# One order of work for the attention stage: mix, halves, late tiles and rotation move

## The chip, the cores and the metric

The kernel runs on one core of a Trainium2 chip. The metric is the device time of one execution in microseconds; before the change it is 2108.4 us, the median of three runs (2104.35 to 2110.85). Nothing about the result is known where this part of the document was written.

## The reference

Two layers of a hybrid decoder. Each normalises x, projects it with one matrix, runs sliding window attention (group A) and retention (group B) beside each other, gates both and projects back. Only group A matters here. Cut to that:

```
h = rms_norm(x, norm_g);  p = h @ w_in                      # 2048 prompt rows + 32 sample rows
qa = rotary(rms_norm(qa, q_norm_g), pos, 16, 500000)        # 8 heads of 64
ka = rotary(rms_norm(ka, k_norm_g), pos, 16, 500000)        # 2 heads of 64
s  = (qa @ ka.T) * 64 ** -0.5, masked to a window of 128    # own block and the one before
p  = exp(s - m) / (sum(exp(s - m)) + exp(sink - m))
attn = p @ va;   mixed = concat(silu(ga) * attn, ...)       # x = x + mixed @ w_out
```

## The kernel before

A layer has four stages in time: A, B0, B1 (two heads of the retention each) and O (the projection back). Each goes over 17 steps, one of 32 sample rows and 16 tiles of 128 prompt rows. Every product of the projections is made of three f16 products (a high part and a low part of each operand), so every operand is written twice: by ScalarE (ACT) the high part, by another engine the low part. Every engine has its own order of instructions, written out by hand, and semaphores between them. The A stage of layer 0 also makes the tiles of h that are missing at its start.

In step s of stage A the engines hold three tiles at once: s is projected, t = s-1 gets its scores and softmax, u = s-2 its product with v and its gate ("mix"). In one step:

- TensorE (PE) runs `proj` in three pieces (q of 512 columns, k and v of 256, gate of 512), 24, 24 and 24 matmuls. In between stand `a_T` (transposes of q and k of t, 18 matmuls into piece 0), `a_S` for both key groups (in the middle of piece 1), `a_PV(u,0)` (before piece 2) and `a_PV(u,1)` (18 matmuls into piece 2). `a_T` waits for the rotated q and k (`a_qk`), and for both mixes of the tile before (`a_mx`), because it writes into the bank TK that the second mix reads.
- ScalarE copies the transposed q and k as f16 (`a_tout`), takes squares of q (`a_q`) and k (`a_kv`), the exponentials of both halves (`a_exp`), the high parts of the probabilities (`a_phi`), of v (`a_vhigh`) and the tanh of the gate (`a_tanh`). That last one waits for `a_mx` too.
- VectorE (DVE) follows with `gate`, the low parts (`a_plo` of the probabilities, `a_vlow` of v, `a_lo` of q and k), `a_land_q` and `a_land_k` (q and k out of PSUM), `a_softmax(t,0)` and `(t,1)` (mask, maximum), the twelve links of the reciprocal root (`a_norm_link`), `a_rotate` and the two mixes.
- SyncE (SP) issues the DMAs: `prob_T(s,g)` transposes the probabilities of half g (it waits for `a_plo`), `store_mix` writes the mix, `p_T(n)` transposes tile n of h. `a_softmax(t,1)` waits (`a_tp`) until `prob_T(u,1)` has landed, since it writes where that transposition reads from.
- GpSimd (POOL) issues the loads of the weights, does the reduction of a maximum over partitions (`share_max`), and in layer 0 the low parts of the tiles 4 to 16 of h (`late_low`). `load_weights` and `share_max` stand between them.

In steps 8 to 15 ("weight steps") DVE and ACT also split the next weights: `w_high` and `w_low`, two each in a step. Steps 4 to 6 have maxima of these weights (`w_absmax`, then `w_top`) at their end. The others are called plain here. In the trace, DVE's L1004 is `gate`, L1017 `a_plo`, L1010 `a_vlow`, L930 `a_land_q`, L1051 the mask of the softmax, L972 the scaling at the head of `a_rotate`, L981 to L984 its rotation, L889 `w_low`, L1112 the mixes; PE's L569 and L571 are `a_T`, L605 `a_S`, L645 `a_PV`; POOL's L1988 and L1990 are `late_low`; SP's L2097 is `prob_T`, L2057 `store_mix`, L2089 `p_T`; ACT's L1788 is the high part of a tile of h.

## Time and profile before

| | |
|---|---|
| median of three runs | 2108.4 us |
| the profiled execution | 2112.67 us |
| its span, first to last instruction | 2110.7 us |
| busy: PE, DVE, ACT, POOL | 1837.4, 1407.4, 715.7, 134.4 us |
| mean granted TensorE clock | 0.947 |
| stage A of layer 0 and of layer 1 | some 65 to 515 us, some 1140 to 1520 us |

Busy time is a share of the span and says nothing of what an engine waits for. A row of a timeline is one instruction or several merged ones, and where the engine was idle before it the row ends with that time and with whoever released it. Outside stage A the order of no engine changes.

### The profile page before, as it was taken

What the parts mean: (1) busy time and instruction counts of PE and PEld (TensorE: products, weight loads), DVE (VectorE), ACT (ScalarE), POOL (GpSimd) and SP (SyncE); (2) the same over time, 40 slices, a digit from 0 to 9 for tenths busy, and PEclk for the clock granted to TensorE, in tenths of its full rate; (3) what the DMA queues carried; (4) which work ended last, traced back from release to release, by engine and by line L of the source; (5) the groups of instructions that cost most, each with busy time, mean ns of one, the idle gap of its engine ahead of it and who ended that gap; (6) DMA issues with size and microseconds to landing.
All of it is one profiled execution on the core that took longest, in us unless ns stands there. A gap on an engine that the chain in (4) does not pass through costs nothing.

```text
span 2110.7 us, 36140 instructions
## 1 busy us (share of the span) xinstructions
PE 1837.4 (87%) x11752; PEld 1004.8 (48%) x11752; DVE 1407.4 (67%) x4699; ACT 715.7 (34%) x1809; POOL 134.4 (6%) x134
## 2 busy tenths in 40 slices
PE   0787677795899999997899988898599999999999
PEld 0344344453455555553344555454255555555444
DVE  4768577783666576667786799888376657667442
ACT  2544344452122222222243455555112222232110
POOL 3221122101000000003001000001000000000000
PEclk9888888898899999999999999999799999999999
DMA  5953233327200120019999133234610021002874
GB/s 148 226 137 70 51 73 75 71 59 169 77 11 10 64 88 12 10 41 252 223 247 232 22 76 75 56 68 87 121 49 13 10 92 59 10 12 77 189 216 148
DMA packets 353803, 196.64 MB, mean 93 GB/s; under 512 B 296624, under 2 KB 327536, under 8 KB 353552
## 3 DMA queue, kind: packets, MB, share of 16 engines
q1 hardware_dynamic: 343984, 159.89, 32.6%
q0 software_dynamic: 9728, 35.66, 5.4%
q8 instruction: 42, 0.69, 0.1%
q14 instruction: 49, 0.40, 0.1%
HBM read 88.75 MB, written 41.16 MB: 62 GB/s over the span
## 4 chain that ended last, share of the span: by engine, by line
PE 53%; DVE 19%; DMA 8%; issue 6%; ACT 3%; SPq 3%; POOL 2%; DVEq 1%; ACTq 0%; POOLq 0%
PE PB L515 22%; PE PA L515 21%; DMA r<-r 5%; DVE r L1051 3%; DVE mix L1112 2%; PE S L669 1%; PE OB L688 1%; PE TK L658 1%; PE S L704 1%; PE OB L695 1%; DVE r L1017 1%; DVE land L972 1%; POOL hT L1988 1%; DMA hT<-land 1%; DVE w_mx L872 1%
## 5 line engine op out<-in xcount | busy, mean ns | idle before, releaser
L515 PE MATMUL PA<-w_a,hT 128*128 128x512 f16 (+1 forms) x1920 | 416.0, 368 | 18.2 <-DVE land L1004 16.9
L515 PE MATMUL PB<-w_a,hT 128*128 128x512 f16 (+1 forms) x1920 | 422.3, 372 | 8.1 <-DVE land L946 4.6
L515 PEld LDWEIGHTS PB<-w_a,hT 128*128 (+1 forms) x1920 | 190.5, 102 | 200.5 <-issue 30.8
L515 PEld LDWEIGHTS PA<-w_a,hT 128*128 (+1 forms) x1920 | 189.2, 101 | 199.4 <-issue 20.9
L515 PE MATMUL PA<-w_b,hT 128*128 128x512 f16 x768 | 184.4, 392 | 21.5 <-DVE land L1004 21.5
L515 PE MATMUL PA<-w_b,r 128*128 128x512 f16 x768 | 174.9, 385 | 24.0 <-DMA r<-r 15.1
L515 PE MATMUL PB<-w_b,hT 128*128 128x512 f16 x768 | 180.8, 386 | 3.9 <-DVE r L1141 3.9
L1680 ACT ACTIVATE r<-r,nm,unqk 128x256 f32<-128x256 f32 x256 | 149.9, 589 | 67.3 <-DVE sd L1064 67.3
L515 PE MATMUL PB<-w_b,r 128*128 128x512 f16 x768 | 171.3, 379 | 0.0
L1745 ACT ACTIVATE r<-OB 128x128 f32<-128x128 f32 (+1 forms) x136 | 36.3, 272 | 390.5 <-PE S L704 364.1
L1161 DVE TENSOR_TENSOR r<-S,t_dec 128x256 f32<-128x256 f32 x64 | 27.2, 424 | 159.1 <-PE S L669 158.9
L515 PEld LDWEIGHTS PA<-w_b,r 128*128 128x128 f16 x768 | 75.1, 99 | 119.9 <-DMA r<-r 24.3
L515 PEld LDWEIGHTS PA<-w_b,hT 128*128 (+1 forms) x768 | 76.4, 101 | 111.7 <-DVE land L1004 22.0
L515 PEld LDWEIGHTS PB<-w_b,r 128*128 128x128 f16 x768 | 75.0, 98 | 90.1 <-DVE r L1263 0.9
L515 PEld LDWEIGHTS PB<-w_b,hT 128*128 (+1 forms) x768 | 75.8, 99 | 84.2 <-issue 5.5
L1051 DVE CUSTOM_DVE_ANT_0 r<-X,t_ma 128x256 f32<-128x256 f32 x128 | 46.7, 421 | 84.5 <-DMA r<-r 82.9
L1017 DVE SCALAR_TENSOR_TENSOR r<-r 128x1024 f16<-128x1024 f32 x64 | 79.2, 1237 | 13.3 <-ACT r L1695 13.3
L1757 ACT ACTIVATE r<-r,minv 128x1024 f16<-128x1024 f32 (+1 forms) x34 | 39.1, 1149 | 142.3 <-DVE minv L1224 135.7
L645 PE MATMUL TK<-r 128*128 128x64 f16 x768 | 29.5, 198 | 47.9 <-DMA r<-r 47.9
L1192 DVE SCALAR_TENSOR_TENSOR r<-r,S 128x128 f32<-128x128 f32 x120 | 29.1, 284 | 62.5 <-PE S L704 62.2
L541 PE MATMUL PA<-w_a,hT 128*32 128x256 f16 (+1 forms) x336 | 22.0, 343 | 54.1 <-DVE w_a L889 53.3
L1695 ACT ACTIVATE r<-r 128x1024 f16<-128x1024 f32 x64 | 67.3, 1051 | 1.0
(254 smaller groups left out, 2843.8 us busy)
## 6 DMA issues: line engine op xcount, KB each, us to landing
out<-r SPq DMA_DIRECT2D x40, 512.0 KB, 4.6
r<-mixed SPq DMA_DIRECT2D x32, 512.0 KB, 4.0
w_b<-in_w_in POOLq DMA_DIRECT2D x16, 512.0 KB, 8.8
mixed<-mix SPq DMA_DIRECT2D x32, 256.0 KB, 2.9
w_a<-in_w_in POOLq DMA_DIRECT2D x16, 512.0 KB, 13.2
mixed<-mix SPq DMA_DIRECT2D x64, 128.0 KB, 1.8
w_b<-in_w_out POOLq DMA_DIRECT2D x16, 512.0 KB, 7.4
r<-in_x_prompt SPq DMA_DIRECT2D x16, 512.0 KB, 4.7
```

What stands on the lines that cost most here:

```text
L515: last = nc.tensor.matmul(out[0:s.rows, 0:n], lhs, w16(ph, k, p, wpart), start=(k == 0 and part == 0 and wpart == 0), stop=(k == KT - 1 an ...
L541: last = nc.tensor.matmul(quarter(ph, j)[:, 0:CH_A[j][1] if ph == "A" else 256], lhs, w, start=(k == 0 and part == 0 and wpart == 0), stop ...
L645: last = nc.tensor.matmul(OO[g][:, h * A_DIM:(h + 1) * A_DIM], pT16[g][:, e, o:o + P], v16[:, q, ve, h // 2 * A_DIM:(h // 2 + 1) * A_DIM], ...
L1017: V.scalar_tensor_tensor(out=ph16[g][:, 1, :], in0=prob_t[g], scalar=P_TOP, in1=ph16[g][:, 0, :], op0=ALU.mult, op1=ALU.subtract).then_inc ...
L1051: return V.tensor_tensor_reduce(out=prob_t[g][:, h * 256:(h + 1) * 256], in0=(SS, XX)[g][h // 2][:, (h % 2) * 256:(h % 2) * 256 + 256], in ...
L1112: last = V.scalar_tensor_tensor(out=mix[:, b, m:m + A_DIM], in0=OO[g][:, o:o + A_DIM], scalar=rr[:, g, h:h + 1], in1=land[:, b, A_W + 2 * ...
L1161: V.tensor_tensor(stm, S0[:, 0:256], t_dec[:, h:h + 2, :].rearrange("p h n -> p (h n)"), ALU.mult).then_inc(b_dm, 1)
L1192: last = V.scalar_tensor_tensor(out=x, in0=x, scalar=lam(h0 + h) ** P, in1=S1[:, h * P:(h + 1) * P], op0=ALU.mult, op1=ALU.add)
L1680: A.activation(x, x, ACT.Exp, scale=unqk[:, 0:1], bias=nm[:, g, h:h + 1], accum_out=rsum[:, g, h:h + 1])
L1695: A.activation(ph16[g][:, 0, :], prob_t[g], ACT.Copy, scale=P_TOP).then_inc(a_ph, 1)
L1745: last = A.activation(osq[0:r, h * P:(h + 1) * P], OB[0:r, h * P:(h + 1) * P], ACT.Square, accum_out=oss[0:r, h:h + 1])
L1757: A.activation(mh_of(s)[0:r, 0, :], mxt[0:r, b, :], ACT.Copy, scale=minv[0:r, b:b + 1]).then_inc(o_hi, 1)
```

## The change

It has five parts, all in stage A.

1. On DVE the second mix (`a_mix(u,1)`, four instructions) moves from the end of the step into the chain of the reciprocal root; both mixes are now taken apart, one instruction between two links. `w_low(k,1)` moves from the chain to the end.
2. `a_lo` (low parts of q and k) and `a_land_q` come ahead of `a_plo(u,1)` and `a_vlow`; on ACT `a_tout` and `a_q` come ahead of `a_phi(u,1)` and `a_vhigh`.
3. The low parts of tiles 4 to 16 of h go from POOL to DVE (`p_low`, one instruction each instead of two), behind `a_step`.
4. On SP the late tiles' transposition `p_T(c+4)` stands at the end of step c; it stood at the head of step c+1, ahead of `prob_T(.,1)`. Five of the nine late loads of x come after step 2. `store_mix` comes ahead of `prob_T(.,0)`.
5. The four rotation instructions go from DVE to POOL (`a_rope`), in all 17 steps of both layers. `load_weights` for B0 and `share_max` now stand behind the rotations of their step.

DVE, step 16 of layer 1, from the gate of tile t to the mask of the first half, before. `r<-r 128x1024` is `a_plo(u,1)`, `kT_lo` and `r<-TK` are `a_lo`, `land<-PA` is `a_land_q`:

```order
2416 L1004 SCALAR_TENSOR_TENSOR land<-land,PB 128x512
2417 L1017 SCALAR_TENSOR_TENSOR r<-r 128x1024
2418 L1076 TENSOR_TENSOR rr<-rsum,es 128x4
2419 L1010 SCALAR_TENSOR_TENSOR r<-land,cs_A,r 128x128
2420 L1079 RECIPROCAL rr<-rr 128x4
2421 L990 SCALAR_TENSOR_TENSOR kT_lo<-S,qk_s,kT_hi 128x128
2422 L992 SCALAR_TENSOR_TENSOR r<-TK,qk_s,r 128x512
2423 L1083 TENSOR_SCALAR rr<-rr,cs_A 128x4
2424 L1076 TENSOR_TENSOR rr<-rsum,es 128x4
2425 L930 SCALAR_TENSOR_TENSOR land<-PA,cs_A,qk_g 128x512
2426 L934 TENSOR_REDUCE ss<-r 128x8
2427 L1079 RECIPROCAL rr<-rr 128x4
```

The same place in the changed kernel:

```order
2705 L993 SCALAR_TENSOR_TENSOR land<-land,PB 128x512
2706 L1065 TENSOR_TENSOR rr<-rsum,es 128x4
2707 L979 SCALAR_TENSOR_TENSOR kT_lo<-S,qk_s,kT_hi 128x128
2708 L981 SCALAR_TENSOR_TENSOR r<-TK,qk_s,r 128x512
2709 L1068 RECIPROCAL rr<-rr 128x4
2710 L930 SCALAR_TENSOR_TENSOR land<-PA,cs_A,qk_g 128x512
2711 L934 TENSOR_REDUCE ss<-r 128x8
2712 L1072 TENSOR_SCALAR rr<-rr,cs_A 128x4
2713 L1006 SCALAR_TENSOR_TENSOR r<-r 128x1024
2714 L1065 TENSOR_TENSOR rr<-rsum,es 128x4
2715 L999 SCALAR_TENSOR_TENSOR r<-land,cs_A,r 128x128
2716 L1068 RECIPROCAL rr<-rr 128x4
```

`a_plo(u,1)` went from second place to ninth, behind both large instructions of `a_lo` and `a_land_q`.

DVE at the end of a weight step of layer 1, before: the scaling, the rotation, `a_plo(t,0)` and the second mix.

```order
2402 L972 TENSOR_TENSOR land<-land,rs 128x640
2403 L192 REGISTER_ALU
2404 L981 ISA
2405 L981 TENSOR_TENSOR r<-land,t_rap 128x160
2406 L982 ISA
2407 L982 TENSOR_TENSOR r<-land,t_rap 128x160
2408 L192 REGISTER_ALU
2409 L983 TENSOR_TENSOR land<-r 128x10x8
2410 L984 TENSOR_TENSOR land<-r 128x10x8
2411 L1017 SCALAR_TENSOR_TENSOR r<-r 128x1024
2412 L192 REGISTER_ALU
2413 L1112 SCALAR_TENSOR_TENSOR mix<-TK,rr,land 128x64 x4
```

And in the changed kernel:

```order
2696 L855 SCALAR_TENSOR_TENSOR rs<-rt,rs 128x10
2697 L192 REGISTER_ALU
2698 L972 TENSOR_TENSOR land<-land,rs 128x640
2699 L1006 SCALAR_TENSOR_TENSOR r<-r 128x1024
2700 L888 REGISTER_ALU
2701 L889 ISA x2
2702 L889 SCALAR_TENSOR_TENSOR w_b<-w_b,w_gs 128x512
```

Behind the scaling now stand `a_plo(t,0)` and `w_low`; rotation and mix are gone from here.

POOL around the reduction in step 6 of layer 0, in the changed kernel with its waits. The ISA rows without a tile load the code for what follows:

```order
52 L2024 TENSOR_TENSOR r<-land,t_rap 128x160 [waits a_qk_normed,a_qk_ready]
53 L2025 TENSOR_TENSOR r<-land,t_rap 128x160
54 L2027 TENSOR_TENSOR land<-r 128x10x8 [waits chain_rope]
55 L2028 TENSOR_TENSOR land<-r 128x10x8
56 L2009 ISA [waits w_max]
57 L2009 ISA w_am<-w_m 128x1
58 L2024 ISA [waits a_qk_normed,a_qk_ready]
59 L2024 TENSOR_TENSOR r<-land,t_rap 128x160
60 L2025 TENSOR_TENSOR r<-land,t_rap 128x160
61 L2027 TENSOR_TENSOR land<-r 128x10x8 [waits chain_rope]
```

The instruction that brings the code back (row 58) stands behind the wait for the scaled q and k of step 7, not ahead of it.

The diff, cut to its core:

```diff
+                V.tensor_tensor(x, x, y.unsqueeze(2).broadcast_to([r, A_HEADS + A_KV, A_DIM]), ALU.mult
+                                ).then_inc(a_nm, 1)
                 ch.end()
...
+                        a_lo(L, t)
                         a_rr_link(u, 0, m0, 1)
-                        a_lo(L, t)
+                        a_land_q(L, s)
                         a_rr_link(u, 0, m0, 2)
+                        a_plo(L, u, 1)
...
+                        a_mix_open(L, u, 0, m0)
+                        a_mix_head(u, 0, 0)
                         a_norm_link(s, ch, 0)
-                        a_mix(L, u, 0, m0)
+                        a_mix_head(u, 0, 1)
                         a_norm_link(s, ch, 1)
...
+                        a_mix_open(L, u, 1, m1)
+                        a_mix_head(u, 1, 0)
                         a_norm_link(s, ch, 6)
...
                         a_rotate(L, s, ch)
                         a_plo(L, t, 0)
-                        a_mix(L, u, 1, m1)
+                        if k is not None:
+                            w_low(L, "B0", k, 1)
...
+                def late_h(c):
+                    if c == 0:
+                        p_rstd(1)
+                        p_low(4)
+                        p_low(5)
...
+                    if 4 <= c <= 12:
+                        p_low(c + 4)
...
-            def late_low(n):
-                alone(pool, x_hi, n + 1)
-                G.tensor_scalar(x_of(n), x_of(n), py[:, n:n + 1], None, ALU.mult).then_inc(ch_late, 1)
-                alone(pool, ch_late, n - 3)
-                G.tensor_tensor(xh_of(n, 1), x_of(n), xh_of(n, 0), ALU.subtract).then_inc(x_lo, 1)
+            def a_rope(L, s):
+                r, b, c = s.rows, s.par, an(L, s)
+                alone(pool, a_nm, c + 1)
+                if c > 0:
+                    alone(pool, a_qk, c)
...
+                G.tensor_tensor(rp1[0:r, :, :, :], both, cos, ALU.mult)
+                G.tensor_tensor(rp2[0:r, :, :, :], both, sin, ALU.mult).then_inc(ch_rope, 1)
+                alone(pool, ch_rope, c + 1)
+                G.tensor_tensor(xa, rp1[0:r, :, 0, :], rp2[0:r, :, 1, :], ALU.subtract)
+                G.tensor_tensor(xb, rp1[0:r, :, 1, :], rp2[0:r, :, 0, :], ALU.add).then_inc(a_qk, 1)
...
                     for c in range(2, STEPS):
-                        if 5 <= c <= 13:
-                            p_T(c + 3)
                         a_step(Step(c))
+                        if c == 2:
+                            for n in range(PRO + 4, STEPS):
+                                load_px(n)
+                        if 4 <= c <= 12:
+                            p_T(c + 4)
```

## Rows read from the trace of the kernel before

**Rows 1.** Engines' busy us (and instructions) in a stretch; granted clock, DMA share, GB/s.
```profile
340.00:400.00 60.00, 45.94 (x352) 26.54 (x353) 43.31 (x139) 29.84 (x68) 14.91 (x6) 0.86 0.36 74
```
**Rows 2.** Chain of waits, layer 0, one step: start us, us, what.
```profile
288.51 1.15 ACT r L1788
...
289.85 2.85 POOL hT L1988
...
296.99 4.75 DMA r<-r
```
**Rows 3.** SP's timeline, layer 0: the stores of the mix close a step each.
```profile
174.10 1.23 SPq L2057 DMA_DIRECT2D mixed<-mix  x1
...
224.81 1.15 SPq L2057 DMA_DIRECT2D mixed<-mix  x1
...
263.17 1.07 SPq L2057 DMA_DIRECT2D mixed<-mix  x1
...
289.17 1.00 SPq L2057 DMA_DIRECT2D mixed<-mix  x1
...
476.48 1.13 SPq L2057 DMA_DIRECT2D mixed<-mix  x1
```
**Rows 4.** POOL's timeline around the reduction, layer 0 (start us, us, idle before).
```profile
233.44 0.38 POOL L1983 PARTITION_ALL_REDUCE w_am<-w_m  x1 [26.05 <-issue]
...
240.52 2.85 POOL L1988 TENSOR_SCALAR hT<-hT,py 128x1024 f32<-128x1024 f32 x1 [6.70 <-issue]
```
**Rows 5.** PE's timeline, layer 1, one weight step.
```profile
1349.30 0.33 PE L569 MATMUL S<-eye,land 128*128 128x128 f32 x1 [2.06 <-DVE mix L1112]
...
1350.00 2.76 PE L515 MATMUL PB<-w_a,hT 128*128 128x512 f16 x6
...
1354.29 0.28 PE L605 MATMUL S<-kT_hi,r 64*128 64x256 f16 x2
```
**Rows 6.** DVE's timeline, the same step.
```profile
1353.61 0.74 DVE L930 SCALAR_TENSOR_TENSOR land<-PB,cs_A,qk_g 128x512 f32<-128x512 f32 x1
1354.27 0.67 DVE L934 TENSOR_REDUCE ss<-r 128x8 f32<-128x512 f32 x1
...
1357.75 0.42 DVE L1051 CUSTOM_DVE_ANT_0 r<-X,t_ma 128x256 f32<-128x256 f32 x1
...
1363.29 0.75 DVE L889 SCALAR_TENSOR_TENSOR w_b<-w_b,w_gs  x1 [1.09 <-ACT w_b L1610]
...
1365.79 0.82 DVE L972 TENSOR_TENSOR land<-land,rs 128x640 f32<-128x640 f32 x1
...
1367.67 1.22 DVE L1017 SCALAR_TENSOR_TENSOR r<-r 128x1024 f16<-128x1024 f32 x1
1368.81 0.85 DVE L1112 SCALAR_TENSOR_TENSOR mix<-TK,rr,land 128x64 f32<-128x64 f32 x4
```
**Rows 7.** Line L2097 (`prob_T`), layer 1: from issue to landing.
```profile
DMA to landing us min/median/max: 4.2/4.3/6.0
```
**Rows 8.** POOL's and DVE's timelines, layer 0, at one time.
```profile
205.26 2.13 POOL L1990 TENSOR_TENSOR r<-hT,r 128x1024 f16<-128x1024 f32 x1 [0.18 <-POOL hT L1988]
...
205.31 2.23 DVE L1010 SCALAR_TENSOR_TENSOR r<-land,cs_A,r 128x128 f16<-128x128 f32 x1
```
**Rows 9.** The same two engines at another time.
```profile
91.98 0.82 DVE L972 TENSOR_TENSOR land<-land,rs 128x640 f32<-128x640 f32 x1
...
92.20 2.58 POOL L1990 TENSOR_TENSOR w_b<-w_b 128x1024 f16<-128x1024 f32 x1 [0.18 <-POOL w_b L1988]
```
**Rows 10.** SP's timeline, layer 1: stores of the mix, steps 3 and 16.
```profile
1214.71 1.11 SPq L2057 DMA_DIRECT2D mixed<-mix  x1
...
1470.39 1.14 SPq L2057 DMA_DIRECT2D mixed<-mix  x1
```
**Rows 11.** ACT's timeline, layer 0, squares of k in step 2.
```profile
124.62 0.37 ACT L1636 ACTIVATE r<-PB,cs_A 128x128 f32<-128x128 f32 x1 [13.95 <-DMA out<-land]
```
**Rows 12.** PE's timeline, layer 1, first transposes of the sample tile.
```profile
1152.99 0.28 PE L555 MATMUL TK<-eye,land 32*64 32x32 f32 x4 [2.65 <-DVE land L984]
```

More of the change, by code:

```diff
@@ L1109, in a_mix, with a_mix_open, a_mix_head @@
                     for h in range(A_GROUP):
-                        o = h * A_DIM
-                        m = (h // 2 * A_GROUP + 2 * g + h % 2) * A_DIM
-                        last = V.scalar_tensor_tensor(
-                            out=mix[:, b, m:m + A_DIM], in0=OO[g][:, o:o + A_DIM],
-                            scalar=rr[:, g, h:h + 1], in1=land[:, b, A_W + 2 * KV_W + m:A_W + 2 * KV_W + m + A_DIM],
-                            op0=ALU.mult, op1=ALU.mult)
+                        last = a_mix_head(s, g, h)
                     last.then_inc(a_mx, 1)
                 ch.end()
+            def a_mix_open(L, s, g, ch):
+                ch.wait()
+                v.wait_ge(a_pv, 2 * an(L, s) + g + 1)
+                if g == 0:
+                    v.wait_ge(mix_out[s.par], 16 * mix_count("A", L, s))
+                ch.end()
+            def a_mix_head(s, g, h):
+                b, o = s.par, h * A_DIM
+                m = (h // 2 * A_GROUP + 2 * g + h % 2) * A_DIM
+                return V.scalar_tensor_tensor(
+                    out=mix[:, b, m:m + A_DIM], in0=OO[g][:, o:o + A_DIM],
+                    scalar=rr[:, g, h:h + 1], in1=land[:, b, A_W + 2 * KV_W + m:A_W + 2 * KV_W + m + A_DIM],
+                    op0=ALU.mult, op1=ALU.mult)
             def b_rope(ph, L, s):
@@ L1381, in a_step @@
                     else:
-                        a_plo(L, u, 1)
                         m0 = a_rr(L, u, 0)
                         a_rr_link(u, 0, m0, 0)
-                        a_vlow(L, u)
+                        a_lo(L, t)
                         a_rr_link(u, 0, m0, 1)
-                        a_lo(L, t)
+                        a_land_q(L, s)
                         a_rr_link(u, 0, m0, 2)
+                        a_plo(L, u, 1)
                         m1 = a_rr(L, u, 1)
                         a_rr_link(u, 1, m1, 0)
-                        a_land_q(L, s)
+                        a_vlow(L, u)
                         a_rr_link(u, 1, m1, 1)
@@ L1423, in a_step @@
                         a_plo(L, t, 0)
+                def late_h(c):
[3 more added lines that the diff above has]
+                        p_low(5)
+                    if c == 1:
+                        p_low(6)
+                        p_low(7)
+                    if c in (2, 4):
+                        p_rstd(c // 2 + 1)
+                    if 4 <= c <= 12:
+                        p_low(c + 4)
                 for c in range(CVA):
@@ L1440, in layer @@
                         w_scale(L, "B0")
-                with v.Fori(0, KT // 2) as i:
-                    for c in (0, 1):
-                        a_step(Step(CVA + c, i), c + 2 * i)
+                if L == 0:
+                    for c in range(CVA, CVA + KT):
+                        a_step(Step(c), c - CVA)
+                        late_h(c)
+                else:
+                    with v.Fori(0, KT // 2) as i:
+                        for c in (0, 1):
+                            a_step(Step(CVA + c, i), c + 2 * i)
                 for c in range(CVA + KT, STEPS):
@@ L1450, in layer @@
                 gate("A", L, E, 2, A_W, A_W + 2 * KV_W)
-                a_plo(L, E - 1, 1)
                 m0 = a_rr(L, E - 1, 0)
                 a_rr_link(E - 1, 0, m0, 0)
+                a_lo(L, E)
+                a_rr_link(E - 1, 0, m0, 1)
+                a_plo(L, E - 1, 1)
+                a_rr_link(E - 1, 0, m0, 2)
                 a_vlow(L, E - 1)
-                a_rr_link(E - 1, 0, m0, 1)
-                a_lo(L, E)
-                a_rr_link(E - 1, 0, m0, 2)
                 m1 = a_rr(L, E - 1, 1)
@@ L1831, in a_step @@
                         a_pout(L, u, 1)
-                    else:
+                    a_tout(L, t)
+                    a_q(L, s)
+                    if not u.sample:
                         a_phi(L, u, 1)
                         a_vhigh(L, u)
-                    a_tout(L, t)
-                    a_q(L, s)
                     if k is not None:
@@ L2145, in _ @@
                 p_T(3)
-                for n in range(PRO, STEPS):
+                for n in range(PRO, PRO + 4):
                     load_px(n)
```

56 lines of the change are left out of this document (22 added, 34 removed).

## The prediction

> **What bounds the kernel now.** I read the windows of the whole span first. In stages B and O TensorE is nearly always busy; stage A is where it waits: in a stretch of layer 0 it works 45.9 of 60 us, at a granted clock of 0.86, while GpSimd works 14.9 [rows 1]. The change touches stage A alone, so the question is how long one of its steps takes in each layer.
>
> Second, SyncE's timeline, where each store of a mix closes a step. Twelve steps of layer 0, 5 to 16, take 476.48 - 174.10 = 302.4 us; an ordinary one of those that make a late tile of h takes 289.17 - 263.17 = 26.0, and one takes 263.17 - 224.81 = 38.4 [rows 3]. In layer 1 the thirteen steps 4 to 16 take 1470.39 - 1214.71 = 255.7, 19.7 each [rows 10]. What differs is the late tile.
>
> Third, the chain of waits shows why: high part of h on ScalarE, 2.85 us on GpSimd, a second GpSimd instruction (2.13 us for its shape [rows 8]), the transposition of h issued, and only then, on the same queue, the transposition of probabilities that the softmax waits for, 4.75 [rows 2]. Two GpSimd instructions sit in the loop of every such step, though nobody needs that tile for three more steps. The step of 38.4 us holds the reduction: GpSimd sat idle 6.7 between it and its next instruction without a releaser, loading code, and in the idle 26.05 before the reduction there is a load of the same kind [rows 4].
>
> Fourth, one weight step of layer 1, the cleanest loop. With the start of `a_T` (1349.30) as zero: `a_land_q` at +4.3, second softmax half at +8.45, scaling at +16.5, `a_plo(t,0)` at +18.4, second mix from +19.5 to +20.4; then `a_T` again [rows 5, 6]. TensorE idled 2.06 before it. VectorE is the chain, nearly without a gap.
>
> **The late tiles (parts 3 and 4).** The 2.85 + 2.13 on GpSimd and the issue of the h transposition leave the loop. On VectorE one `p_low` of the shape of `a_plo`, 1.22 [rows 6], comes in. It stands behind the step, waits for ScalarE's tanh and high part, and is followed by the gate; I cost it at nothing because VectorE then waits in the new loop anyway (below). Without that cover it costs 1.2 in each of nine steps, 11 us. The transposition of h now flies before the one of the probabilities and is gone when that is issued. So layer 0 becomes like layer 1, and the rest is what a step of layer 1 becomes.
>
> **The loop after the change (parts 1, 2, 5).** Take the weight step again, zero at `a_T`. TensorE's matmuls behind it ran slowly there (six of 512 columns in 2.76 us, 0.46 each, the lower clock of 1.2 GHz, after an idle time of 2.06 [rows 5]). In the new loop it will idle longer before `a_T`, so I keep that. The squares of q wait for those six, so `a_land_q` stays at +4.3 and its reduction ends at +5.6 [rows 6]. Only now comes `a_plo(u,1)`: 1.22, +6.9. Its transposition lands 4.3 after the issue [rows 7], with two hand-overs +11.5. The second half of the softmax writes where that transposition reads: before it started at +8.45 without a wait, now it starts at +11.5. This wait is new and costs VectorE 3.0.
>
> From there to the end of the scaling took 1366.61 - 1357.75 = 8.9 us before. Out of it goes the wait of 1.09 for ScalarE and one `w_low` of 0.7 [rows 6]. Two mixes in single instructions (0.85 for four) fit mostly into the links' waits and cost together about what one did in a lump. So 6.9, and the scaling ends at +18.4.
>
> Then the rotation on GpSimd. No row shows it. Below it is bounded by what VectorE needed, 1.06 between scaling (1366.61) and `a_plo` (1367.67) [rows 6]. By the large row, 2.13 us for 1024 columns [rows 8], its 160, 160, 80 and 80 columns are 1.0, with the 0.18 between dependent instructions [rows 8] 1.2. Above: four times the 0.38 of the smallest GpSimd instruction here [rows 4] on top, 2.7. I take 1.6, near the large row with a tenth for each instruction.
>
> And it has to get at its data. VectorE's `a_vlow`, normally 0.34, took 2.23, until GpSimd's tensor_tensor of 2.13 was over [rows 8]; and GpSimd's took 2.58 instead of 2.13 when it began inside a VectorE tensor_tensor of 0.82 [rows 9]. They exclude each other both ways. VectorE issues `a_plo(t,0)`, with two operands in SBUF, right behind the scaling, so I let GpSimd wait until it is over, 1.2.
>
> The Trainium skill ("GPSIMD Engine Reference", section 1, Specifications) says that the two engines share their SBUF interfaces and contend when a VectorE instruction reads two SBUF inputs. That is a rule against this change; rows 8 and 9 agree. Without it each step would be 1.2 shorter, which is a rival below.
>
> Sum: 18.4 + 1.2 + 1.6 + 0.1 = +21.3 for a weight step (20.4 before in layer 1), and 0.7 less, 20.6, for a plain one. The maxima of steps 4 to 6, late in the step, hide in the wait before `a_T`. What part 1 takes off TensorE's waits (tanh and gate no longer stand behind the second mix) comes back as one longer wait before `a_T`.
>
> **The reduction and the load of code.** Until now layer 1 had no tensor instruction on GpSimd and needed no reload. Now step 7 in both layers and step 0 in both layers begin with one, and it stands behind the wait for the scaled tile. 6.7 [rows 4] instead of the 1.2 of hold-up: +5.5 for each step 7.
>
> **The sums**, against the profiled execution of 2112.7 us (span 2110.7; the median is 4.3 lower):
>
> - Layer 0, steps 5 to 16: four plain at 20.6, eight weight steps at 21.3, and 5.5: 258.3 instead of 302.4: -44.
> - Layer 0, start: squares of k in step 2 waited 13.95 for small stores queued behind the late transpositions, until 124.6 [rows 11]. The lows of tiles 4 to 7 no longer cost 5 us each on GpSimd, and five large loads are out of the way. But the first rotation pays a reload. I take -8, bounds -13 and 0. The five loads, now issued in the way of step 3, give back 3. Steps 3 and 4: +1.
> - Layer 1, steps 4 to 16: 5 x 20.6 + 8 x 21.3 + 5.5 = 278.9 instead of 255.7: +23.
> - Layer 1, steps 2 and 3, plain: +4 for both.
> - Layer 1, start: the sample tile's transposes waited for the rotation already [rows 12]; with the reload they come 7 later, of which a wait for the last tile of h hides a part: +5.5.
> - End of stage A: `a_plo(E-1,1)` stands behind `a_lo` and its transposition behind more of the load of the next weights: +2 a layer, +4.
>
> -44 - 8 + 3 + 1 + 23 + 4 + 5.5 + 4 = -11.5, so 2101 in the profile and 2096.5 for a median. Layer 0 gains, layer 1 loses.
>
> **Rivals.**
>
> B, GpSimd is not held up: it gets in between scaling and `a_plo`, or waits for nothing. For it: in rows 9 it had to wait only for the rest of one instruction. Against: VectorE has nothing to wait for behind the scaling. About 25 steps gain 1.2, and 0.2 with a rotation at its 1.2: -35, 2062.
>
> C, the slower side: the rotation costs 2.7 us and one `w_low` (0.7, two SBUF operands) gets in between its instructions. Every step is 1.8 longer, 25 x 1.8 = 45, 2141. For it: the bound above, and the exclusion of rows 8. It decides from 0.5 us a step on, where the gain of 11.5 is used up; layer 1 is then over 35 us slower and layer 0 no longer pays for it.
>
> C2, between A and C: GpSimd needs twice VectorE's 1.06 [rows 6], 2.1, as it does in the large (2.13 for 1024 columns, `a_plo` 1.22 [rows 8, 6]). The step is 0.5 longer than mine, 25 x 0.5 = 12.5, and the result is 2109, no change. The Trainium skill ("GPSIMD Engine Reference", section 4.1, Engine selection) gives the same factor for two inputs and advises VectorE for such work.
>
> D, the change doesn't do what it says: `p_low` on VectorE waits for ScalarE behind tanh, and SyncE's issue of `p_T` still delays the probabilities, so late steps stay at 26. Then only layer 1's loss is left: about 2145. Against: three steps of slack, and in the new order `p_T` is issued some 5 us before `prob_T(.,1)`.
>
> E, the landing of the transposition does not bite, because `a_plo(u,1)` comes earlier than I say (a fast clock, squares of q earlier): 2.2 less in each of 25 steps, 2041.
>
> **How the numbers follow.** My forecast A 0.40, B 0.22, C 0.20, C2 0.08, D 0.05, E 0.05. Changes of under 0.3%, 6 us, can't be told from none. Faster: 0.29 of A, B and E: 0.56. Same: 0.07 of A and 0.05 of C2: 0.12. Slower: C, D, 0.04 of A and 0.03 of C2: 0.32. The range goes from just under B, 2055, to C, 2140; A by itself, with the start of layer 0 and 0.4 a step either way, is 2083 to 2112.
>
> **What would show it.** The stores of the mix: steps of layer 0 from 26 to about 21, those of layer 1 from 19.7 to about 21. VectorE's mask of the second half (L1040 then) waiting 2 to 3 us for a DMA in every step. TensorE's wait before `a_T` released by GpSimd instead of VectorE, 3 to 4 us. GpSimd's first rotation instruction longer than its second by what it is held up. Near 7 us between the wait and the rotation in steps 0 and 7. I am wrong if a step of layer 1 gets shorter than before, or if the rotation takes over 2.2 us.

## The result: a little slower

| | before | after |
|---|---|---|
| median | 2108.5 us (20 runs) | 2125.5 us (20 runs) |
| the profiled execution | 2112.7 us | 2119.8 us |
| its span | 2110.7 us | 2117.9 us |
| busy: PE, DVE, ACT, POOL | 1837.4, 1407.4, 715.7, 134.4 us | 1843.7, 1359.4, 722.7, 159.2 us |

The ratio of the times is 1.008, 95% interval 1.0066 to 1.0093. I had forecast 2096.5 and faster; the time is 29 us above that, inside the range and on the other side of no change. The two profiled executions lie only 7 us apart, where the medians lie 17 apart: the one before is 4 us above its median, the one after 6 below. So the comparison of the two traces by stretch accounts for 7 us and not for the 17. One of the six executions of a kernel further down (parts 1, 3, 4 with all loads of x early) took 3316.5 us at a granted clock of 0.68 and is left out of its median.

SyncE's stores of the mix in the changed kernel, layer 0 (sample tile, steps 3, 4 and 16, last tile), answer to [rows 3] (start us, us, what):

```profile
121.51 0.32 SPq L2089 DMA_DIRECT2D mixed<-mix  x1
154.23 0.38 SPq L2089 DMA_DIRECT2D mixed<-mix  x1
177.21 0.36 SPq L2089 DMA_DIRECT2D mixed<-mix  x1
452.69 0.33 SPq L2089 DMA_DIRECT2D mixed<-mix  x1
495.06 0.33 SPq L2089 DMA_DIRECT2D mixed<-mix  x1
```

Layer 1, sample tile, steps 3 and 16, last tile, answers to [rows 10]:

```profile
1179.09 0.32 SPq L2089 DMA_DIRECT2D mixed<-mix  x1
1198.73 0.35 SPq L2089 DMA_DIRECT2D mixed<-mix  x1
1488.40 0.33 SPq L2089 DMA_DIRECT2D mixed<-mix  x1
1529.61 0.34 SPq L2089 DMA_DIRECT2D mixed<-mix  x1
```

And those of the kernel before that [rows 3, 10] don't hold:

```profile
131.71 0.32 SPq L2057 DMA_DIRECT2D mixed<-mix  x1
154.99 1.00 SPq L2057 DMA_DIRECT2D mixed<-mix  x1
518.28 0.33 SPq L2057 DMA_DIRECT2D mixed<-mix  x1
1195.95 0.32 SPq L2057 DMA_DIRECT2D mixed<-mix  x1
1518.16 0.34 SPq L2057 DMA_DIRECT2D mixed<-mix  x1
```

From these, the difference by stretch:

| stretch | forecast | the two traces |
|---|---|---|
| layer 0, up to the sample tile's store | -8 | -10.2 |
| layer 0, step 3 and step 4 | +1, and +3 for the x loads | +9.4 and +3.9 |
| layer 0, steps 5 to 16 | -44 | -26.9 (275.5 against 302.4) |
| layer 0, end of stage A | +2 | +0.6 |
| from there to the sample tile's store in layer 1 | +5.5 | +6.4 |
| layer 1, step 3 | part of +4 | +0.9 |
| layer 1, steps 4 to 16 | +23 | +34.0 (289.7 against 255.7) |
| layer 1, end of stage A, and the rest | +2 | -6.6 and -4.2 |
| sum | -11.5 | +7.2 |

Of the -6.6 at the end of stage A in layer 1 some 4 are not the change's: in the kernel with parts 3 and 4 alone, whose layer 1 is that of before, the stretch takes 43.6 us and not 47.8.

Now one weight step of layer 1, the same whose counterpart is in [rows 5, 6]. TensorE:

```profile
1383.03 0.47 PE L569 MATMUL S<-eye,land 128*128 128x128 f32 x1 [4.08 <-POOL land L2028]
...
1384.15 2.77 PE L515 MATMUL PA<-w_a,hT 128*128 128x512 f16 x6
```

VectorE, from the scaling of the step before it to its own:

```profile
1378.70 0.82 DVE L972 TENSOR_TENSOR land<-land,rs 128x640 f32<-128x640 f32 x1
1379.44 1.22 DVE L1006 SCALAR_TENSOR_TENSOR r<-r 128x1024 f16<-128x1024 f32 x1
1380.58 1.01 DVE L889 SCALAR_TENSOR_TENSOR w_b<-w_b,w_gs  x1
...
1387.67 0.75 DVE L930 SCALAR_TENSOR_TENSOR land<-PA,cs_A,qk_g 128x512 f32<-128x512 f32 x1 [1.21 <-ACT r L1645]
...
1389.06 1.22 DVE L1006 SCALAR_TENSOR_TENSOR r<-r 128x1024 f16<-128x1024 f32 x1
...
1394.85 0.42 DVE L1040 CUSTOM_DVE_ANT_0 r<-X,t_ma 128x256 f32<-128x256 f32 x1 [1.81 <-DMA r<-r]
...
1401.22 0.82 DVE L972 TENSOR_TENSOR land<-land,rs 128x640 f32<-128x640 f32 x1
```

GpSimd, its rotation between the two:

```profile
1379.80 1.24 POOL L2024 TENSOR_TENSOR r<-land,t_rap 128x160 f32<-128x160 f32 x1 [19.43 <-DVE land L972]
1381.00 0.96 POOL L2025 TENSOR_TENSOR r<-land,t_rap 128x160 f32<-128x160 f32 x1
1382.14 0.35 POOL L2027 TENSOR_TENSOR land<-r 128x80 f32<-128x80 f32 x1 [0.18 <-POOL r L2025]
1382.45 0.35 POOL L2028 TENSOR_TENSOR land<-r 128x80 f32<-128x80 f32 x1
```

The reader is to see four things. The wait for the landing is there (1.81 before the mask; `prob_T` was issued only after `a_plo` ended at 1390.28). GpSimd's first instruction takes 1.24 where an undisturbed one takes 0.51 or 0.52 (the run without a VectorE instruction beside it, below), because VectorE has `a_plo` in hand (1379.44 to 1380.66), and the second 0.96, because `w_low` got in between; that `w_low` took 1.01 itself instead of 0.75. From the end of the scaling to the end of the rotation it is 3.28. And TensorE waits 4.08 for it and then runs six matmuls of 512 columns in 2.77; the granted clock of that stretch is 0.50, the lower of its two levels.

Over the whole trace the waits for the rotation and for the landing are about equal (engine and line, released by: us in total, times, longest):

```profile
PE S L569 <- POOL land L2028: 104.3, 28, 8.8
DVE r L1040 <- DMA r<-r: 102.4, 31, 13.3
```

Before, the mask had its waits for landings too, fewer and longer, most of them in layer 0. So by the total the second wait has grown by 20 us only; in the weight steps of layer 1 it is new:

```profile
DVE r L1051 <- DMA r<-r: 82.9, 12, 22.4
```

The stretch of layer 0 that [rows 1] show, in the changed kernel:

```profile
340.00:400.00 60.00, 48.60 (x402) 28.86 (x399) 45.17 (x162) 32.61 (x79) 10.02 (x12) 0.91 0.36 75
```

TensorE works 48.6 us of the 60 instead of 45.9: layer 0 gained, as forecast.

### The profile page after: what moved, and what is told of

Its sections match the earlier page's. It is cut to its first block, busy times and chain, and to the rows that moved or that the text cites. A ratio compares the mean times of both kernels' runs of the same rounds, so it can differ in the third digit from the quotient of the medians.

```text
span 2117.9 us, 35845 instructions
## 1 busy us (share of the span) xinstructions
PE 1843.7 (87%) x11752; PEld 1012.7 (48%) x11752; DVE 1359.4 (64%) x4576; ACT 722.7 (34%) x1809; POOL 159.2 (8%) x244
## 4 chain that ended last, share of the span: by engine, by line
PE 56%; DVE 18%; DMA 11%; issue 5%; POOL 4%; SPq 3%; ACT 2%; DVEq 0%; POOLq 0%; ACTq 0%
PE PB L515 23%; PE PA L515 22%; DMA r<-r 9%; DVE r L1040 2%; DVE mix L1115 2%; DVE r L1006 2%; POOL r L2024 1%; PE S L669 1%; PE OB L688 1%; PE TK L658 1%; PE S L704 1%; PE OB L695 1%; DVE land L972 1%; POOL r L2025 1%; DVE w_mx L872 1%
## 5 line engine op out<-in xcount | busy, mean ns | idle before, releaser
L515 PE MATMUL PA<-w_a,hT 128*128 128x512 f16 (+1 forms) x1920 | 420.9, 372 | 8.1 <-DVE land L993 7.9
L515 PEld LDWEIGHTS PA<-w_a,hT 128*128 (+1 forms) x1920 | 191.8, 102 | 190.3 <-issue 20.3
L515 PE MATMUL PA<-w_b,hT 128*128 128x512 f16 x768 | 181.2, 387 | 21.3 <-DVE land L993 21.3
L515 PEld LDWEIGHTS PA<-w_b,r 128*128 128x128 f16 x768 | 75.9, 100 | 117.9 <-DMA r<-r 21.3
L515 PEld LDWEIGHTS PA<-w_b,hT 128*128 (+1 forms) x768 | 75.6, 99 | 109.1 <-DVE land L993 21.8
L569 PE MATMUL S<-eye,land 128*128 128x128 f32 x32 | 12.8, 400 | 106.9 <-POOL land L2028 104.3
L2024 POOL TENSOR_TENSOR r<-land,t_rap 128x160 f32<-128x160 f32 x32 | 34.6, 1082 | 608.3 <-DVE land L972 574.9
L541 PE MATMUL PA<-w_a,hT 128*32 128x256 f16 (+1 forms) x336 | 22.4, 346 | 53.9 <-DVE w_a L889 53.0
```

What stands on the lines that cost most here:

```text
L515: last = nc.tensor.matmul(out[0:s.rows, 0:n], lhs, w16(ph, k, p, wpart), start=(k == 0 and part == 0 and wpart == 0), stop=(k == KT - 1 an ...
L541: last = nc.tensor.matmul(quarter(ph, j)[:, 0:CH_A[j][1] if ph == "A" else 256], lhs, w, start=(k == 0 and part == 0 and wpart == 0), stop ...
L2024: G.tensor_tensor(rp1[0:r, :, :, :], both, cos, ALU.mult)
```

## The experiments

The parts were taken off one by one or in groups, and then three repairs were tried on the changed kernel. "Part" counts as in the list of the change; a weight step is the mean by the stores of layer 1, steps 9 to 15. "Parts 3 and 4 alone" has of part 4 only the place of `p_T`; the loads of x and the store stay as before. Where part 5 is undone, GpSimd's loads of the B0 weights go out early again too.

| kernel | median | ratio to before (95%) | weight step |
|---|---|---|---|
| before | 2105.7 to 2109.4 | 1 | 20.3 |
| parts 3 and 4 alone | 2060.4 | 0.976 (0.972 to 0.980) | 20.3 |
| parts 1, 3, 4 | 1995.5 | 0.946 (0.942 to 0.949) | 16.9 |
| parts 1 to 4 | 2031.5 | 0.963 (0.960 to 0.965) | 19.1 |
| parts 1, 3, 4, 5 | 2060.4 | 0.977 (0.974 to 0.979) | 20.3 or 18.6 each |
| all five (after) | 2125.5 | 1.008 (1.007 to 1.009) | 22.2 |

Part 5, the rotation on GpSimd, costs 94 us beside part 2 and 65 without it. Part 2, the late `a_plo(u,1)`, costs 36 and, beside part 5, 65. Parts 3 and 4 gain 48, part 1 some 53 more (with five loads of x late, whose place made no clear difference there), and the store's place 12. Parts 3 and 4 were not told apart.

### Part 5 undone: rotation on VectorE

```diff
-                V.tensor_tensor(x, x, ...).then_inc(a_nm, 1)
+                ch(V.tensor_tensor(x, x, ...))
+                V.tensor_tensor(rp1[0:r, :, :, :], both, cos, ALU.mult)
+                ch(V.tensor_tensor(rp2[0:r, :, :, :], both, sin, ALU.mult))
+                V.tensor_tensor(xa, rp1[0:r, :, 0, :], rp2[0:r, :, 1, :], ALU.subtract)
+                V.tensor_tensor(xb, rp1[0:r, :, 1, :], rp2[0:r, :, 0, :], ALU.add).then_inc(a_qk, 1)
...
-                    a_rope(L, Step(c))
```

> The changed kernel with the four rotation instructions back on VectorE, parts 1 to 4 kept. Theory 1 (the rotation on GpSimd is what costs): in the changed kernel 3.28 us lie between the end of the scaling and the end of the rotation in a weight step of layer 1, against 1.06 on VectorE; 2.2 us less in each of some 28 steps is 62 us, and the two reloads of code in step 7 and that at the start of layer 1 give another 15: 2125 - 77 = about 2048, steps of layer 1 near 20.2 instead of 22.4. Theory 2 (the late low part of the probabilities and the landing behind it are what costs): only the difference of the own times, 1.85 - 1.06 = 0.8 in 28 steps, and the reloads go: about 2090. Rival: what VectorE takes over it loses again, since the waits before a_T only change their releaser: 2115 to 2125.

2031.5 us, 94 less than after, more than the first theory asked. TensorE and VectorE in a weight step of layer 1 of this kernel:

```profile
1305.92 0.32 PE L568 MATMUL S<-eye,land 128*128 128x128 f32 x1 [2.01 <-DVE land L983]
...
1306.52 1.46 PE L514 MATMUL PA<-w_a,hT 128*128 128x512 f16 x6
```
```profile
1309.06 0.72 DVE L929 SCALAR_TENSOR_TENSOR land<-PA,cs_A,qk_g 128x512 f32<-128x512 f32 x1
...
1316.20 0.42 DVE L1050 CUSTOM_DVE_ANT_0 r<-X,t_ma 128x256 f32<-128x256 f32 x1 [1.91 <-DMA r<-r]
```

The step is 3.4 shorter than the usual 22.4 of after: 2.2 is the rotation (3.28 against 1.06), 1.3 is the clock (2.77 against 1.46 for the same six matmuls), and with both `a_land_q` starts 3.1 behind `a_T` instead of 4.6. The wait for the landing stays at 1.9: it is part 2's.

### Part 2 undone: a_plo(u,1) early, rotation on GpSimd

```diff
+                        a_plo(L, u, 1)
                         m0 = a_rr(L, u, 0)
...
-                        a_plo(L, u, 1)
...
-                    a_tout(L, t)
-                    a_q(L, s)
-                    if not u.sample:
-                        a_phi(L, u, 1)
-                        a_vhigh(L, u)
+                    else:
+                        a_phi(L, u, 1)
+                        a_vhigh(L, u)
+                    a_tout(L, t)
+                    a_q(L, s)
```

> The changed kernel with part 2 undone alone: a_plo(u,1) and a_vlow ahead of a_lo and a_land_q again on VectorE, a_phi and a_vhigh ahead of a_tout and a_q on ScalarE; rotation still on GpSimd. Theory 2: the wait of the second half's mask for the landing (102.4 us over 31 waits in the changed kernel, of which 1.8 in a weight step of layer 1) goes, though q and k come up to 1.5 later: 25 steps shorter by 1.5 to 2.5, 2065 to 2090. Theory 1: the mask waits then for something else, at most 0.5 a step is left: 2112 or more. Rival: the step gets longer, because ScalarE's a_tout comes later by the two instructions ahead of it: over 2130.

2060.4 us, 65 less and below the 2065 to 2090 of the second theory. The waits for a landing fell from 31 to 9. Two steps of this kernel, one behind the other, TensorE:

```profile
1331.47 0.33 PE L569 MATMUL S<-eye,land 128*128 128x128 f32 x1 [1.92 <-POOL land L2028]
...
1333.85 2.66 PE L515 MATMUL PB<-w_a,hT 128*128 128x256 f16 x12
...
1351.74 0.32 PE L569 MATMUL S<-eye,land 128*128 128x128 f32 x1 [1.94 <-POOL land L2028]
...
1353.63 1.47 PE L515 MATMUL PA<-w_a,hT 128*128 128x256 f16 x12
```

The same work, the same wait, and twelve matmuls once at 1.2 GHz and once at 2.4 (granted clock 0.55 and 1.00 in those stretches); the first step took 20.3 us, the second 18.6. So the clock alone is worth 1.7 us a step here. The stall is not cured either: `a_plo(u,1)` now runs while GpSimd rotates, and one of the 80 column instructions takes 1.38 us instead of 0.35. The step gets shorter all the same, since VectorE waits less for landings (53.8 us in all instead of 102.4).

### No VectorE instruction beside the rotation

```diff
                         a_rotate(L, s, ch)
+                        v.wait_ge(a_qk, an(L, s) + 1)
                         a_plo(L, t, 0)
```

> The changed kernel, in which VectorE's a_plo(t,0) waits for the end of the rotation, so that no VectorE instruction works beside GpSimd's four. Theory of the exclusion: the rotation then takes its undisturbed 1.85 us instead of 3.28, a_T starts 1.3 earlier in some 25 steps, 2125 - 32 = about 2093; w_low and a_plo come later by 0.6 and hide in VectorE's wait for a_tout. Rival: 3.28 is the cost of the hand-over and of GpSimd itself, not of the exclusion: 2120 to 2128. If a_plo(t,0) then is late for its transposition and a_PV(u,0), slower: over 2130.

2126.8 us, no gain, and by that number the theory of the exclusion would have fallen. The trace says otherwise. Steps 9 to 16 of layer 1 are 20.4 in the mean, against 22.1 in after, and the rotation takes 0.52, 0.52, 0.35, 0.35. But step 4 takes 34.3. GpSimd and VectorE there:

```profile
1200.70 3.03 POOL L486 DMA_DIRECT2D w_b<-in_w_in  x4
```
```profile
1223.80 0.42 DVE L1040 CUSTOM_DVE_ANT_0 r<-S,t_ma 128x256 f32<-128x256 f32 x1 [17.14 <-DMA r<-r]
```

As soon as the rotation is over GpSimd issues four loads of weights, and the transposition of what `a_plo(t,0)` writes now comes behind them. So I moved the loads where they stood before the change.

```diff
+                    if c == 2:
+                        pool.wait_ge(dve_piece, L * PIECES + PIECE0["A"] + 1)
+                        load_weights(G, "B0", L)
                     a_rope(L, Step(c))
-                    if c in (2, 3):
-                        load_weights(G, "B0", L, range(4 * c - 8, 4 * c - 4))
```

> The run in which VectorE waits for the rotation (2126.8 us measured), with GpSimd's eight loads of the next weights ahead of the rotation of step 2, as they stood before the change, and not behind the rotations of steps 2 and 3. In that run the steps 8 to 15 of layer 1 fell from 22.4 to 20.6 us, but step 4 took 34 us in both layers, VectorE waiting 17 us for a landing behind loads issued 1 us before. If those loads alone ate the gain, step 4 goes back to 22 in both layers: 2127 - 23 = about 2104, which leaves 20 us as the worth of the exclusion. Rival: step 4 is long for another reason, or the loads only collide with the transposition of another step: 2120 to 2130.

2098.4 us: step 4 is 20.2 in layer 0 and 19.6 in layer 1, less than the 23.0 and 22.3 of after. GpSimd in a weight step of this kernel, and TensorE behind it:

```profile
1333.21 0.52 POOL L2025 TENSOR_TENSOR r<-land,t_rap 128x160 f32<-128x160 f32 x1 [18.17 <-DVE land L972]
1333.69 0.52 POOL L2026 TENSOR_TENSOR r<-land,t_rap 128x160 f32<-128x160 f32 x1
...
1334.69 0.35 POOL L2029 TENSOR_TENSOR land<-r 128x80 f32<-128x80 f32 x1
```
```profile
1335.88 1.46 PE L515 MATMUL PB<-w_a,hT 128*128 128x512 f16 x6
```

Undisturbed the rotation is 1.83 us, and the exclusion was worth 1.7 in a weight step (which includes that TensorE has its full clock in part of the steps). The hold has a price of its own, though: steps 5 to 7 are 4 us longer in all in each layer (65.4 against 61.4 in layer 1). So the 27 us of this run are the exclusion, less that, and the loads of weights.

### Late loads of x, and the code loaded ahead

All nine loads of x ahead of step 2, as before the change:

```diff
-                for n in range(PRO, PRO + 4):
+                for n in range(PRO, STEPS):
```

> The changed kernel with all nine late loads of x ahead of step 2 on SyncE, as before the change. In the changed kernel SyncE is held 17.5 us by the five loads behind step 2 and step 3 takes 32.7 us against 23.3. Theory 3 (that block costs what step 3 shows): step 3 is 9 us shorter and steps 0 to 2 as in the changed kernel: about 2116. Rival: the small stores of the sample's k and v queue behind the loads again and squares of k in step 2 wait for them, so what step 3 gives is lost before: 2123 to 2130.

2110.0 us (ratio to before 0.9995, 0.9974 to 1.0016), 15 less than after. In after SyncE sits on the five loads, and the transposition that it has to issue next is issued 17.5 us later, at 143.12:

```profile
125.38 17.54 SPq L2114 DMA_DIRECT2D hT<-in_x_prompt  x5
143.12 4.38 SPq L2129 DMA_TRANSPOSE r<-r  x1
```

VectorE waits for it:

```profile
149.27 0.42 DVE L1040 CUSTOM_DVE_ANT_0 r<-X,t_ma 128x256 f32<-128x256 f32 x1 [13.35 <-DMA r<-r]
```

With the loads early step 3 takes 20.2 instead of 32.7, and the sample tile's store is only 0.8 later (122.3).

The late loads of x are only half of this cause. In after GpSimd issues four loads of weights right ahead of them, behind its rotation (start us, us, what):

```profile
123.09 3.20 POOL L486 DMA_DIRECT2D w_b<-in_w_in  x4
```

In the run above in which all eight loads of weights go out before the rotation of step 2 (at 110.95), the same five late loads of x hold SyncE half as long:

```profile
130.14 8.54 SPq L2116 DMA_DIRECT2D hT<-in_x_prompt  x5
```

Step 3 of layer 0 is 24.0 there instead of 32.7, and 24.0 too with the rotation on VectorE (SyncE held 8.6). So it takes both, late loads of x and late loads of weights, and moving either one takes most of it away.

A small instruction behind each reduction that a rotation follows:

```diff
+                if kind in ("A", "B0"):
+                    G.tensor_tensor(warm[:, :], ones[:, :], ones[:, :], ALU.mult)
```

> The changed kernel with one small tensor_tensor on GpSimd right behind each reduction that a rotation follows, so that the code for it is loaded while GpSimd would wait anyway. If the reload stood in the way, the step of the reduction (28.2 and 28.8 us against 22.9 and 22.4) and the first rotation of layer 1 lose it: 5 to 6 us in each of three places, 2125 - 16 = about 2109. Rival: those steps are long for another reason (w_scale and w_top on VectorE, which the kernel before has too, or the landing): 2120 to 2128.

2106.7 us, 19 less. GpSimd in layer 0:

```profile
242.82 0.20 POOL L2012 TENSOR_TENSOR warm<-ones 128x8 f32<-128x8 f32 x1 [6.86 <-issue]
245.58 1.24 POOL L2027 TENSOR_TENSOR r<-land,t_rap 128x160 f32<-128x160 f32 x1 [2.56 <-DVE land L973]
```

The load of code (6.86 with what stands around it) now lies in time in which GpSimd waits anyway; in after the first rotation instruction behind the reduction stood at 254.86, behind an idle time of 16.90 that ended with the load. The step concerned falls from 28.2 to 22.5 in layer 0 and from 28.8 to 22.7 in layer 1; the third place is the start of layer 1, which comes 4.9 sooner behind the last store of layer 0. The Trainium skill ("GPSIMD Engine Reference", section 2.1, Instruction dispatch) tells that the first call into freshly loaded code pays about 6 us that no instruction of the profile shows, and the trace agrees.

All three repairs together (no VectorE instruction beside the rotation, loads of weights and of x early, code ahead):

> The same as the run beside it, with the code loaded ahead behind the reduction and all late loads of x ahead of step 2. If the repairs add up (19 us for the code, 15 for the loads of x, both measured on the changed kernel), 2104 - 34 = about 2070, still 40 above the 2031.5 with the rotation on VectorE, because GpSimd's 1.85 against 1.06, two hand-overs and the lower clock of TensorE in each step stay. If the loads of x and of the weights were one and the same collision, only the first counts: 2085.

2066.2 us: they add up (2098.4 less 19 and 15 is 2064). It is still 35 above the rotation on VectorE; a weight step of layer 1 is 20.5 against 19.1.

### What the rest of the change is worth

Parts 3 and 4 alone on the kernel before (loads of x and `store_mix` as before):

```diff
+                if L == 0:
+                    for c in range(CVA, CVA + KT):
+                        a_step(Step(c), c - CVA)
+                        late_h(c)
...
-                        if 5 <= c <= 13:
-                            p_T(c + 3)
                         a_step(Step(c))
+                        if 4 <= c <= 12:
+                            p_T(c + 4)
```

> The kernel before with parts 3 and 4 alone: low parts of the late tiles of h on VectorE, their transposition issued at the end of a step on SyncE; the nine loads of x and the place of store_mix stay as before. Nothing else of the order changes. If the late tiles' path is what made layer 0 slower than layer 1 (26 against 20 us a step), layer 0 goes to near 21 a step: eight steps of 5 less and 10 at the reduction, 2108 - 55 = about 2053. Rival (rival D of the prediction): ScalarE's high part behind tanh and VectorE's wait for it keep the steps at 26: 2100 to 2110.

2060.4 us. Weight steps of layer 0 fall from 26 to 21.4, step 7 from 38.4 to 22.8. Layer 1 is unchanged, 20.3. What a late tile still costs is not the difference of the two, because the clock is low in the weight steps of layer 1 and full in those of layer 0 (six matmuls behind `a_T` in 2.6 to 2.8 and in 1.46 us). Within layer 0, at the full clock, steps 9 to 13 with a late tile take 20.7 to 21.8 and steps 14 and 15 without one 19.2 and 18.5: over 2 for a late tile, more than the 1.2 of `p_low` (1.7 in the next kernel, 18.5 against 16.8).

Part 1 on top, that is the changed kernel with parts 2 and 5 undone:

> Parts 1, 3 and 4 of the change: rotation on VectorE, and a_plo(u,1) early on VectorE and ScalarE again, against parts 1 to 4 (2031.5 us measured). If the late a_plo(u,1) costs by its landing also with the rotation on VectorE (the mask still waits 1.9 to 2.0 us in a weight step there), 1 to 2 us in 25 steps go: 1985 to 2005. Rival: with early a_plo the q and k of the scores come later by as much, and the step stays at 19: 2025 to 2040. A second rival: the idle time before a_T stays over 2 us, and TensorE's clock falls there, as in layer 1 of the run with a_plo early (20.3 a step with the clock low, 18.3 with it high): then nothing or a loss in those steps.

1995.5 us, the best so far. TensorE in a weight step of layer 1:

```profile
1277.18 0.60 PE L570 MATMUL TK<-eye,land 128*128 128x128 f32 x4
1277.62 1.46 PE L514 MATMUL PA<-w_a,hT 128*128 128x512 f16 x6
```

No idle time stands before `a_T` any more in these steps, and the clock stays high (granted 1.00 from 1150 to 1370 us). The same stretch of layer 0 as [rows 1]:

```profile
340.00:400.00 60.00, 58.69 (x513) 34.59 (x511) 56.83 (x232) 39.57 (x101) 1.43 (x2) 1.00 0.35 74
```

TensorE works 58.7 of 60 us there at full clock, against 45.9 at 0.86 before and 48.6 at 0.91 in after.

The same with all loads of x early:

> As the run with parts 1, 3 and 4, with all nine late loads of x ahead of step 2. In the changed kernel this gave 15 us, of which some 12 in step 3. With the rotation on VectorE step 3 took 24.0 and not 32.7 though five loads stood behind step 2. If those loads are what delays the transposition in step 3, another 4 to 8 us go; if GpSimd's loads of weights behind its rotation were the other half of that collision, there is nothing left to gain, and the queue of small stores in step 2 costs 0 to 8 us.

1991.9 us (ratio 0.944, 0.939 to 0.948), not told apart from 1995.5. Step 3 falls from 25.4 to 19.2, and the sample tile's store comes 2.6 later. With GpSimd's loads of weights out of the way the place of the loads of x is worth little.

The same as 1995.5 with `store_mix` behind `prob_T(.,0)`:

> Parts 1 and 3 and most of 4 (1995.5 us measured), with store_mix behind prob_T(.,0) on SyncE as before the change. It separates the woven mixes from the place of the store: against the kernel with parts 3 and 4 alone (2060.4, steps of layer 1 at 20.2) that run had both and took 16.9 a step. If the woven mixes are the cause, 1992 to 2000 again. If the store's place had a share, over 2005.

2007.5 us: the store's place has a share, and the mixes are not all. SyncE there:

```profile
1306.33 0.63 SPq L2081 DMA_DIRECT2D mixed<-mix  x1
1307.59 1.84 SPq L2121 DMA_TRANSPOSE r<-r  x1
```

`a_plo(u,1)` had ended at 1306.13; the store stood ahead of its transposition, which was issued 1.5 us later, and VectorE's mask waits for a landing 26 times instead of 14. The two `a_plo` lie only 2.4 us apart in this order, so what stands between their two transpositions counts.

Part 3 undone in the 1995.5 kernel, low parts on GpSimd, the transposition of h one step later:

```diff
-                        if 4 <= c <= 12:
-                            p_T(c + 4)
+                        if 5 <= c <= 13:
+                            p_T(c + 3)
...
+                    if L == 0 and 4 <= c <= 12:
+                        late_low(c + 4)
```

> The run with parts 1, 3 and 4 (1995.5 us), with part 3 undone: the low parts of the late tiles of h are made by GpSimd's two instructions again, and their transposition is issued one step later, still at the end of a step on SyncE, behind prob_T, with two steps of slack left. It separates where the gain of layer 0 is from: the place of the issue on SyncE or the engine. If the issue is all, and VectorE, which is the chain, gets its 1.5 us a step back: steps 8 to 13 of layer 0 at 16.9 instead of 18.5, and layer 0's step of the reduction stays short: about 1985. Rival: GpSimd's tensor_tensor of 2.13 holds VectorE's two-operand instructions off (in the kernel before a_vlow took 2.23 instead of 0.34): steps over 19, 2000 to 2010; and if SyncE stands waiting for the low part in the step of the reduction (GpSimd's 7 us of code), that step is 5 longer.

2066.5 us, a miss beyond both theories. Steps of layer 0 take 27.3, and it is ScalarE that waits, in front of the high part of a late tile:

```profile
317.74 1.15 ACT L1818 ACTIVATE r<-hT,py 128x1024 f16<-128x1024 f32 x1 [9.20 <-DMA hT<-r]
```

The high part of tile n waits until the transposition of tile n-1 has landed, since it writes the same buffer. I had counted the slack from when the tile is needed (three steps on), and not from who wants its buffer. Issued a step later, the transposition of tile c+3 stands in the way of `p_high(c+4)` in the same step, ScalarE waits 9.2, and the copies of q and k behind it are late. So the run does not tell what the engine of the low parts is worth; that stays open. By the trace it is the place of the issue that costs here: a step of layer 0 takes 27.3 and not 18.5, more than the 26 before the change.

## Why the prediction was wrong

**What bounds the kernel, and the late tiles.** Right. Parts 3 and 4 alone gave 48 us at the place named. The cost of `p_low` at nothing was nearly right in after (22.7 to 22.9 a step in layer 0, 22.1 to 22.5 in layer 1). The price of a late tile without the cover was not: over 2 with parts 3 and 4 alone, forecast 1.2.

**The loop after the change, +21.3.** This is the step that failed, by its size: most weight steps of layer 1 took 22.3 to 22.5. In the step above, with the start of `a_T` as zero:

| | forecast | trace |
|---|---|---|
| `a_land_q` starts | +4.3 | +4.64 |
| `a_plo(u,1)` ends | +6.9 | +7.25 |
| mask of the second half | +11.5 | +11.82 |
| scaling ends | +18.4 | +19.0 |
| from there to `a_T` | 2.9 | 3.5 |

Every term is late, and all in one direction; together they make 1.2. They are the squares of q (0.35), the chain of norms and mixes (7.2 instead of 6.9) and hold-up and rotation (3.28 instead of 2.8: my 1.6 was short of the undisturbed 1.83, and `w_low` came in between, as rival C had it). The rotation took 3.0 from its first instruction to its last, over the 2.2 that I had named as a sign of being wrong. It was not 1.2 everywhere: the plain steps 4 to 7 and 16 of layer 1 took 21.1 in the mean, forecast 20.6. In the two traces the loop is 17 above the forecast in steps 5 to 16 of layer 0 and 11 in steps 4 to 16 of layer 1, 28 in all, where the forecast gain was 11.5: this term alone turns the sign. The others together take 9 of it back: steps 3 and 4 of layer 0 took 9 more than forecast, the start of layer 0 2 less, the end of stage A in layer 1 and the rest 13 less, and nothing in my account led to these 13; that part is luck.

**The x loads, +3.** It was +9.4 in step 3 and +3.9 in step 4, against +4 for both with the loads. I had priced the five issues and not that SyncE, held by them for 17.5 us, keeps the next transposition back, nor that GpSimd's loads of weights, put behind the rotation, go out at the same moment. Undoing the first gave 15; with the second undone SyncE is held 8.5. And the loads of x were not what delayed the start of layer 0: the sample tile's store came 10.2 earlier in after (forecast 8) and still 9.4 earlier with all loads of x early.

**The reload.** Right where it was put: 5.5 forecast for a place, 19 measured for three (5.7, 6.1 and 4.9 in the traces).

**The landing of the transposition.** Right: a new wait of 1.8 in a weight step, where I had 2 to 3; over the trace the wait grew from 82.9 to 102.4 us. I took it for the smaller evil, and never asked what the change would be without it. Rival E, in which it does not bite, is what part 2 undone does: 65 us less (I gave that mechanism 55).

**Rivals.** C's mechanism is what happened, except that the hold-up and `w_low` and not GpSimd's own time are the cost: the undisturbed rotation takes 1.83, below its 2.7, so the result lies between my forecast and C's 2141. B was wrong: VectorE is ahead in every step from 3 on, except step 7 with its load of code. The rule of the Trainium skill that I had set against the change ("GPSIMD Engine Reference", section 1) is borne out: 1.24 for the first instruction beside `a_plo`, 0.52 without.

**What I had not weighed at all.** I kept the lower clock behind `a_T` because it was in [rows 5], and took it as given. It was not. With parts 1 to 4 TensorE idles 1.9 to 2.0 us there in most of layer 1's weight steps, hardly less than 2.06, and the six matmuls run at 2.4 GHz in all but one of them; with parts 1, 3 and 4 it does not idle there and they do so in all. Where the clock is low it costs 1.3 us (after against parts 1 to 4) to 1.7 us (the two steps of the early `a_plo(u,1)`) a step. So what part 5 costs is the rotation's delay and, in most steps, the clock behind it. Part 1 takes both the idle time and the low clock out of layer 1's weight steps (20.3 to 17.6 by the stores, with the store's place as before); steps 4 to 16 of layer 1 give 22 of its 53 us and steps 5 to 16 of layer 0 another 22. My sum asked what each edit adds; the five parts together hid that three of them were worth 113 us and the other two cost 130.

Left open: how the 94 us of part 5 split in full. The three repairs give back 19 (the code), 27 (the exclusion and the loads of weights) and 15 (the loads of x, of which the loads of weights had already taken part of step 3); the 35 that remain fit 0.8 a step of own time, the hand-overs and the clock, but no run separates these. Nor is it known what sets the clock at waits of about 2 us.

## What to carry to other kernels

When several edits come in one change, price each by itself and against the kernel without the others: here two edits ate what three had gained. Work moved off a busy engine in the middle of a chain costs what the other engine needs more and what it is held up by the instruction issued next (here 1.24 us instead of 0.52 for its first instruction); look for a place where someone waits anyway. A wait ahead of TensorE's work can cost twice, once as time and once as clock behind it: here the same step with the same wait took 18.6 or 20.3 us. And two groups of loads issued at one moment by two engines hold each other up (SyncE for 17.5 us instead of 8.5).

## What the hardware showed unexpectedly

- The granted clock is not told by one wait alone: 1.92 and 1.94 us of idle time ahead of `a_T`, in two steps of one kernel, were followed by matmuls at 1.2 and at 2.4 GHz.
- A transposition issued 1.5 us after the start of four loads of weights was waited for 17.1 us, though SyncE and GpSimd issued them separately; its usual landing takes 4.2. The Trainium skill ("DMA: Bandwidth & Descriptors", Issuing engines are not separate DMA queues) tells that these end on the same 16 engines; the trace agrees.
- GpSimd holds off more than VectorE's instructions with two SBUF tensors. In the run with the low parts on GpSimd this tensor_scalar of 4 columns (usually 0.22) ended with GpSimd's tensor_tensor (2.13 from 322.12 on):

```profile
322.53 1.75 DVE L1083 TENSOR_SCALAR rr<-rr,cs_A 128x4 f32<-128x4 f32 x1
```
